# RG-LRU gate products of a hybrid decoder layer: 64x64 blocks on the four quarters of TensorE, one operand copied with its halves exchanged, and placed four k tiles later

## The reference, cut to what matters

```python
xc, new_conv_a = causal_dwconv(xa, lru_conv0, conv_a_w, conv_a_b)
xb = xc.reshape(B, T, 16, 64)
r = sigmoid(einsum('btnd,nde->btne', xb, wa).reshape(B, T, D) + ba)
i = sigmoid(einsum('btnd,nde->btne', xb, wx).reshape(B, T, D) + bx)
log_a = -8 * r * softplus(-lam)
a = exp(log_a)
u = sqrt(-expm1(2 * log_a)) * i * xc      # multiplier 1 at position 0
h_t = a_t * h_(t-1) + u_t
branch_a = (h * gelu(ga)) @ w_br_a
```

## Time and profile before

| | |
|---|---|
| median of 3 runs | 1227.42 us (1224.98 to 1228.12) |
| the profiled execution, its time | 1228.72 us |
| its span | 1226.9 us |
| PE busy | 1200.1 us (98%) |
| DVE, ACT, POOL busy | 661.0, 467.1, 159.7 us |
| mean granted TensorE clock | 0.994 |

### The profile page before, as it was taken

The page is one execution under the profiler, slowest core; times in us unless marked ns, Lnnn a source line. Parts: engine busy times, 40 slices in busy tenths (PEclk is TensorE's granted clock), DMA queues, the critical chain, the costliest instruction groups (busy, mean ns, idle before and its releaser), DMA issues.

```text
span 1226.9 us, 21263 instructions
## 1 busy us (share of the span) xinstructions
PE 1200.1 (98%) x8821; PEld 1167.0 (95%) x8821; DVE 661.0 (54%) x1337; ACT 467.1 (38%) x724; POOL 159.7 (13%) x258
## 2 busy tenths in 40 slices
PE   9999999999999999999999999999999999999996
PEld 7999999989998999999999999999999999999995
DVE  6543543534522255665545557888437884388721
ACT  6434434344333356666633444222212222122221
POOL 2264143152140000000100000000100001000031
PEclk9999999999999999999999999999999999999998
DMA  8566245254232223222253222222223222222221
GB/s 238 137 183 171 75 118 146 75 141 124 75 97 65 69 70 86 69 78 61 82 150 91 69 69 71 85 85 86 78 81 86 85 80 80 86 85 77 77 86 49
DMA packets 178980, 117.14 MB, mean 95 GB/s; under 512 B 6932, under 2 KB 170920, under 8 KB 178888
## 3 DMA queue, kind: packets, MB, share of 16 engines
q1 hardware_dynamic: 167456, 87.34, 25.3%
q0 software_dynamic: 11440, 28.79, 8.4%
q10 hardware_dynamic: 10, 0.01, 0.0%
HBM read 107.66 MB, written 8.45 MB: 95 GB/s over the span
## 4 chain that ended last, share of the span: by engine, by line
PE 95%; DVE 2%; ACT 2%; issue 1%; POOL 0%; ACTq 0%; POOLq 0%; DVEq 0%
PE ps L620 63%; PE ps L599 19%; PE ps L750 2%; PE ps L827 1%; PE ps L688 1%; PE ps L714 1%; PE ps L675 1%; PE ps L700 1%; PE ps L728 1%; PE ps L755 1%; PE ps L874 0%; PE ps L642 0%; PE ps L891 0%; DVE x_tok L1326 0%; PE ps L902 0%
## 5 line engine op out<-in xcount | busy, mean ns | idle before, releaser
L620 PE MATMUL ps<-h,w_s 128*128 128x288 f32 x3840 | 518.6, 296 | 0.0
L620 PEld LDWEIGHTS ps<-h,w_s 128*128 128x128 f32 x3840 | 513.4, 189 | 1.2 <-issue 0.2
L947 ACT ACTIVATE w_s<-w_raw 128x1024 fp32r<-128x1024 f32 (+1 forms) x161 | 167.4, 1040 | 383.0 <-PE ps L620 383.0
L1310 DVE TENSOR_TENSOR w_s<-w_raw,w_s 128x1024 fp32r<-128x1024 f32 (+1 forms) x161 | 192.5, 1196 | 197.5 <-ACT w_s L947 196.8
L599 PE MATMUL ps<-w_s,h 128*128 128x384 f32 x1152 | 216.5, 341 | 1.3 <-DVE h L1340 0.8
L599 PEld LDWEIGHTS ps<-w_s,h 128*128 128x128 f32 x1152 | 199.2, 188 | 3.3 <-issue 1.7
L620 PE MATMUL ps<-g_hi,w_s 128*128 128x288 f32 x768 | 136.3, 297 | 1.6 <-DVE g_lo L1742 1.6
L620 PEld LDWEIGHTS ps<-g_hi,w_s 128*128 128x128 f32 x768 | 113.6, 189 | 1.9 <-ACT g_hi L1274 1.8
L620 PE MATMUL ps<-g_lo,w_s 128*128 128x288 f32 x384 | 82.3, 296 | 0.0
L553 POOL DMA_DIRECT2D out<-f_row x12 | 6.2, 517 | 510.3 <-ACT f_row L1281 510.3
L620 PEld LDWEIGHTS ps<-g_lo,w_s 128*128 128x128 f32 x384 | 61.9, 189 | 0.0
(11 more groups left out here) (285 smaller groups left out, 1441.6 us busy)
## 6 DMA issues: line engine op xcount, KB each, us to landing
w_raw<-in_w_in SPq DMA_DIRECT2D x65, 512.0 KB, 4.0
w_raw<-in_w_up SPq DMA_DIRECT2D x48, 512.0 KB, 3.9
w_raw<-in_w_down SPq DMA_DIRECT2D x24, 512.0 KB, 3.8
kc<-in_cache_k_g POOLq DMA_DIRECT2D x48, 128.0 KB, 3.0
vc<-in_cache_v_g POOLq DMA_DIRECT2D x12, 512.0 KB, 5.7
w_raw<-in_w_br_a SPq DMA_DIRECT2D x8, 512.0 KB, 3.9
w_raw<-in_w_out SPq DMA_DIRECT2D x8, 512.0 KB, 3.8
x_tok<-in_x_prompt SPq DMA_DIRECT2D x4, 512.0 KB, 7.4
```

The lines of the kernel that those rows point to most:

```text
L620: last = mm(pu[u % 2][:, 512 * a:512 * a + HALF], w[:, part, k, :], x[:, k, HALF * a:HALF * (a + 1)], start=(k == 0 and i == 0), stop=(k = ...
L947: A(w_s[:, ring(u), 0, 0:nkt[u], :], w_raw[:, u % NRAW, 0:nkt[u], :], ACT.Copy).then_inc(hi_ready, 1)
L1310: TT(w_s[:, ring(u), 1, 0:nkt[u], :], w_raw[:, u % NRAW, 0:nkt[u], :], w_s[:, ring(u), 0, 0:nkt[u], :], ALU.subtract).then_inc(lo_ready, 1)
```

## The change

The matrices `wa` and `wx` keep only their 64x64 blocks, one on partitions 0 to 63 and one on 64 to 127. In `wx` the two blocks' places are exchanged, and so its products read `xsw`, a copy of `xc` with exchanged halves of the partitions, which POOL makes with two DMAs from on-chip memory to on-chip memory in each round. The four products of 300 columns with 128x128 weights become eight with 64x64 weights, in two groups of four, one on each quarter of the array. PE waits for the copy. The gate products stand ahead of k tile 5 instead of k tile 1.

```diff
-        wa = at(o_r + VEC, "wa", [P, KT, P])
-        wx = at(o_r + VEC + 4 * KB, "wx", [P, KT, P])
+        wa = at(o_r + VEC, "wa", [P, KT, LB])
+        wx = at(o_r + VEC + 2 * KB, "wx", [P, KT, LB])
+        xsw = at(o_r + VEC + 4 * KB, "xsw", [P, LW])
...
-            pool.memset(wa[:, :, :], 0.0).then_inc(gw_zero, 1)
-            pool.memset(wx[:, :, :], 0.0).then_inc(gw_zero, 1)
-            pool.wait_ge(gw_zero, 2)
-            for buf, name in ((wa, "lru_wa"), (wx, "lru_wx")):
+            for n, (buf, name) in enumerate(((wa, "lru_wa"), (wx, "lru_wx"))):
                 src = t[name][0].rearrange("(c j) d e -> j d c e", j=2)
                 for j in range(2):
-                    pool.dma_start(buf[64 * j:64 * j + 64, :, 64 * j:64 * j + 64], src[j]).then_inc(gw_in, 16)
+                    p0 = LB * (j ^ n)
+                    pool.dma_start(buf[p0:p0 + LB, :, :], src[j]).then_inc(gw_in, 16)
...
             for c in range(KT):
+                pool.wait_ge(xc_rdy, c + 1)
+                if c:
+                    pool.wait_ge(gate_ps, c)
+                for j in range(2):
+                    pool.dma_start(xsw[LB * j:LB * (j + 1), :], xc[LB * (1 - j):LB * (2 - j), c % 2, :]).then_inc(xsw_in, 16)
                 pool.wait_ge(aa_rdy, c + 1)
...
-                for i, w in enumerate((wa, wx)):
-                    for a in range(2):
-                        last = mm(ps[2 + i][:, 512 * a:512 * a + LW // 2], w[:, c, :],
-                                  xc[:, c % 2, a * LW // 2:(a + 1) * LW // 2], start=True, stop=True)
+                pe.wait_ge(xsw_in, 32 * (c + 1))
+
+                for a in range(2):
+                    cols_ = slice(a * LW // 2, (a + 1) * LW // 2)
+                    for i, (w, x) in enumerate(((wa, xc[:, c % 2, :]), (wx, xsw[:, :]))):
+                        for j in range(2):
+                            rows, o = slice(LB * j, LB * (j + 1)), LB * (j ^ i)
+                            last = mm(ps[2 + i][o:o + LB, 512 * a:512 * a + LW // 2], w[rows, c, :], x[rows, cols_],
+                                      start=True, stop=True)
                 last.then_inc(gate_ps, 1)
...
-                unit(U_LRU + 3 * c + 2, h_hi, h_lo, None, {1: lambda: gate_products(c)})
+                unit(U_LRU + 3 * c + 2, h_hi, h_lo, None, {5: lambda: gate_products(c)})
```

More of the change, by code:

```diff
@@ L36 @@
 C_N = C_SM + 4 * P + NG * NS
+LB = 64
 STRIP, SLOTS = 32, 2
@@ L321, in build @@
         kcT_rdy = [sem("kcT_rdy0"), sem("kcT_rdy1")]
-        gw_zero, gw_in = sem("gw_zero"), sem("gw_in")
+        gw_zero, gw_in, xsw_in = sem("gw_zero"), sem("gw_in"), sem("xsw_in")
         l_link, xa_pad, xc_rdy, gate_ps, l_gr, gate_read = (sem(x) for x in ("l_link", "xa_pad", "xc_rdy", "gate_ps", "l_gr", "gate_read"))
@@ L1564, in linked @@
                 dve.wait_ge(l_link, link[0])
-            dve.wait_ge(gw_zero, 3)
+            dve.wait_ge(gw_zero, 1)
             def conv(c):
```

## The result

The changed kernel takes 1232.39 us in the median of 20 runs, the kernel before 1227.99 in 20 runs beside it. The ratio is 1.0029, with a 95% interval of 1.0018 to 1.0040: 3.6 us slower (2.2 to 4.9), where 1.5 us faster had been forecast. One execution of the changed kernel, which took 2371 us where the other 19 took 1228 to 1238, is left out of the ratio. The profiled execution took 1232.38 us, its span is 1230.6.

The account below looks back on a forecast made before the run. PE, busy 98% of the span, was taken as the bound, with a loop over ACT and DVE just hidden. Terms -7.4 + 3.2 + 3.9 - 1.2 = -1.5 us gave 1225.9 us against the median 1227.42; range 1221.9 to 1236.

Parts of the forecast that it names:

- the length of a round: Recurrence stage, from one tile's gate products to the next: about 20.8 us instead of 21.2.
- a loop over ACT, DVE and the copy: Recurrence stage: xc ready 16.7 us after the gate products' end, PE wants it at 19.2, leaving 2.5 for the copy.
- The copy's way: POOL's wake 0.3, first issue 0.53, landing 2.2, sum 3.0 us; PE waits 0.5 plus waking, 0.55 in seven rounds: +3.9.
- The products on quarters: Gate products on PE: two groups of four take 1.1 us instead of 2.02, saving 0.92 in eight rounds: -7.4 us.
- the link from the products' end to `xc`: ACT and DVE in the recurrence loop: 17.93 us falls to 16.7 as ACT's 1.07 wait and 0.15 lateness drop out.
- Four k tiles later: Start of the recurrence stage: the first gate products come 4 x 0.80 us later, lost once: +3.2 us.
- The end: Last gate products to third half unit: ACT's wait for PE goes, 14.30 becomes 13.06, -1.2 us; PE idles in two pieces.
- No clock loss: PE's half-microsecond gaps ahead of gate products: no clock charge; one drop expected at the end, as today.
- The dropped memsets on POOL: Two memsets and their wait on POOL, ahead of a 52 us pause: removing them gains nothing.
- Row halves that write one bank at different partitions: Rival on gate products: same-bank row halves take turns, 2.0 to 2.5 us instead of 1.1, 1233 to 1237; chance 0.2.
- The late copy: Rival on PE's wait for the copy: 1.5 to 1.75 us each round, 1232.5 to 1234; chance 0.12.
- The hidden copy: Rival on PE's wait: copy there within 2.5 us, sum -5.4 or -6.0, 1221.4 to 1222; chance 0.2.

Follow-up runs that it names:

- e8: Changed kernel with each copy cut from 600 to 150 columns (37.5 KB a DMA instead of 150); round 20.64 us against 21.39, one run.
- e7: Changed kernel without the copy, with each group of quarter products made twice; round 21.56 us, one run.
- e3: Changed kernel without the copy and its wait, wx products reading xc (second gate wrong); round 20.55 us, time ratio to the kernel before 0.9974.
- e4: Changed kernel without copy or exchange, only the two diagonal quarters used, products ahead of k tile 1; round 21.55 us, one run.
- e1: Kernel before with its old gate products only moved ahead of k tile 5; round 21.20 us, time ratio to the kernel before 1.0010.
- e6: Four quarters without copy, ACT exchanging the halves during the tanh, products ahead of k tile 1; 1221.61 us against 1227.91 before, ratio 0.9951.
- e9: Changed kernel with the copy's two DMAs issued side by side, one by POOL and one by SP; round 21.42 us, ratio to before 1.0008.
- e10: Changed kernel, copy included, with its gate products ahead of k tile 1 instead of 5; round 24.46 us, ratio to before 1.0210.
- e5: Changed kernel with both DMAs of the copy issued by SP instead of POOL; round 21.10 us, ratio to before 1.0015.

## Why the prediction was wrong, by its own steps

**What failed** is the length of a round: the forecast had 19.19 + 1.1 + 0.55 = 20.84 us, the trace shows 21.39. Over seven rounds that is 3.9 us, which turns -1.5 into the +2.3 of the trace at the last store. The mechanism, a loop over ACT, DVE and the copy that closes through the gate products, was as forecast, and so were its links; two terms were sized too small. A third cost wasn't in the sum at all: behind the last store the 16 DMAs of POOL take 1.3 us more, and so +2.3 becomes the measured +3.6.

*The copy's way.* "Landing ... I take 2.2" was read from stores of 64 and 96 KB. The copy lands in 2.54 to 2.65 on the chain. Wake 0.28 (0.3 forecast), the step to the second issue about 0.55 (0.53), landing 2.6 (2.2), PE's start 0.13: 3.56 in place of 3.05. e8 shows that size mattered: a quarter of it lands in 1.8. A reading of the nearest row by kind, without its bytes, was 0.4 short, seven times; the two rows themselves, 0.2 us apart for 32 KB, lead to an estimate of 2.4 at 150 KB.

*The products on quarters.* A group is 0.505, at the lower end of what I took (e7). What the forecast had as 0.01 to 0.06 for each group is in truth a price for each visit, 0.35 us (e3, e4, e7). The row of L700 held the hint: 0.19 above the single ones in one visit, which I spread over three groups. For PE's stream the products cost 1.36 and not 1.1, and in the loop 1.27 until ACT can go on. The Trainium skill, TensorEngine Tiling (Array Packing), Key Properties, says that changing the tiling mode drains TensorE. These runs agree in that a change costs, 0.35 us on the way there and back; the forecast cites that page and has no term for this.

The first is worth 0.5 of the 0.55 in a round, the second 0.17, and the link from the products' end to `xc` gave 0.1 back (16.58 in place of 16.7). While PE waits for the copy, the second shows only in the loop's length; e3 shows it alone.

*The end of the program.* The forecast compares the two kernels up to the third half unit and takes the rest as equal. It isn't: POOL's last drain grows from 6.19 to 7.50 us, and the whole stretch behind the last store from 8.99 to 10.31.

**What held.** Four k tiles later: +3.2, measured 3.3. The end: -1.2, measured -1.37, and in two pieces (0.8 and 3.0). No clock loss at gaps of 0.8 us, and one drop at the end as before. The dropped memsets on POOL gave nothing that shows. e1 adds up the place alone to +1.8 in the stage.

**The rivals.** Row halves that write one bank at different partitions do run at once (e4), so the rule that the forecast cites from the Trainium skill, TensorEngine Tiling (Array Packing), Gotcha 1: PSUM Pressure, doesn't hold for this case. The late copy was not the one that I had drawn (1.5 to 1.75 a round): its wait is 0.8. But its half a microsecond, less the 0.1 given back, is already enough for the sign: seven times 0.4 turn -1.5 into +1.3, and the products' 0.17 and POOL's end make the rest. The hidden copy didn't come: with the links as measured it would have needed a way of 20.55 - 1.27 - 16.58 = 2.7 us, and the shortest of a whole copy is SP's 3.2. With a quarter of the data it is 2.8, and the round 20.64.

That the moved place costs and the quarters alone gain is shown (e1, e3, e6). What made the landing on POOL longer with the two copies side by side (e9), and why the end of the program grows with POOL's DMAs, stays open.

## What to carry to other kernels

Before a transfer is put between two engines, add up the loop that it closes: if the consumer's result leads back to the next producer, a later place for the consumer doesn't buy time (though too early a place can make another engine of the loop wait, as in e10), and each tenth of a microsecond of the way is paid in every round. Where a layout has to be exchanged, look for an engine that reads the data anyway and has idle time there. Products on parts of the array are worth their streaming time, and each visit pays once for the change of tiling, so gather many in one visit. And compare two traces to their very end: a cost may stand there that no stage shows.

## What the runs showed of the hardware

- Eight 64x64 products of 300 fp32 columns on four quarters take 1.01 us and 0.35 us for the change there and back, in pairs 2.02 and 0.34; with 128x128 weights four took 2.02 and nothing more (e3, e7, e4, before).
- A copy from on-chip memory to on-chip memory of 64 partitions lands 2.5 us after its issue with 2400 B in each partition and 1.8 us with 600 B; two at once on two queues: 2.5 and 2.9 us.
- SP starts on a DMA 0.02 us after the semaphore of DVE's last step, POOL 0.28 us; the issues of both take about half a microsecond.
- Gaps of 0.8 us of PE in each round left the clock at 1.00, at six of eight gaps of 2.1 to 2.5 us it went to 0.50 for 3.4 or 6.8 us (e10), and the loss was twice the one reckoned without it.
- ACT can read 64 partitions of PSUM and write another 64: 0.76 us, as long as for 128 (e6).
- Each DMA that POOL issued made the drain of POOL at the end of the program 0.08 us longer: 6.19, 6.85, 7.50 and 7.66 us with 0, 8, 16 and 18 more of them; 16 more on SP left it at 6.19 (e5).
